# Attention weights transposed by one DMA inside SBUF instead of by two through DRAM, and the last merge's weights loaded once for both token tiles

## The chip, the cores and the metric

One Trainium2 chip; the same program runs on 8 of its cores, each core on one batch entry (2048 tokens of 1024 channels). The metric is device time in microseconds of the slowest core. Names of engines: PE is TensorE (matmuls), ACT is ScalarE, DVE is VectorE, POOL is GpSimd, SP is SyncE. DMAs that SP issues go to one queue, those that POOL issues to another; both are served by the core's 16 DMA engines.

## The reference, cut to what matters

Two layers; each has a mixer of three gated branches and then a feed-forward block. Here is what the change touches: the attention branch, whose weights w are the difference of two softmaxes, and the gated sum of the branches.

```python
for l in range(DEPTH):
    h = rmsnorm(x, norm_mix_pre[l])
    z = h @ w_in[l]                                  # za | zq | zk | zv | zc | zg
    ya = gmlp_branch(...)
    # branch B, 4 heads, causal: two score maps for each head
    p = jax.nn.softmax(sc, axis=-1)                  # (B,H,2,Q,S)
    w = p[:, :, 0] - lam * p[:, :, 1]                # (B,H,Q,S)
    yb = rmsnorm(einsum('bhqk,bkhe->bqhe', w, v), subln_g) * (1 - lambda_init)
    yc = pool_branch(...)
    up = einsum('bsnw,nwd->bsnd', stack([ya, yb, yc], 2), w_branch[l])
    gates = sigmoid(zg)
    merged = sum(gates * up, axis=2)
    x = x + rmsnorm(merged @ w_out[l], norm_mix_post[l])
    x = x + rmsnorm((silu(g) * u) @ w_ffn_out[l], norm_ffn_post[l])   # g, u from rmsnorm(x) @ w_ffn_in[l]
```

## The kernel before

**Order of work.** The program is written by a planner in Python (class `Sched`, function `emit`): every piece of work is a generator that yields what it needs, and the planner appends the piece that it reckons ready first, by its own durations, to the engine's list. Each engine then runs its list in order and waits on semaphores. So what stands in front of a matmul on PE is fixed beforehand, and a DMA that is later than the planner reckoned stops PE. Streams have priorities: the products with V (`pv_stream`), the scores (`qk_stream`), the output projection (`w_out`), and then the main stream, which fills the rest.

**Attention.** A step is one block of 128 queries (`qb`) of one head; a layer has 64 steps, in the order `ORDER` of blocks, 4 heads each. A step's width is w = (qb+1)*128 keys, from 128 to 2048. PE makes the scores, ACT their exponentials into the rings P (6144 columns, `ring1`) and P2 (3840 columns), DVE scales P2 and adds it to P. The result has queries on partitions, and the product with V needs keys there. `softmax` therefore writes it to DRAM (`wd`, 12 slots) with a DMA of SP, waits, and reads it back with a DMA that transposes blocks of 128 by 128 into the ring WT (8192 columns, `wring`). `pv_stream` gives the product with V a place on PE at the earliest 5 us (`LAG["pv"]`) after the planner's landing time. `finish` normalises a query block, transposes it on PE and sets the flag `("B", l, qb)`.

**Merging.** A slab holds the weights of a gate and a branch for 128 output channels (`dc`, 0 to 7). `gated` makes 8 matmuls for the gate and 4 for the branch, for one tile of 512 tokens. Slabs go through a ring of three slots WS, filled by DMAs of POOL that convert f32 to bf16; `acquire` and `release` count them, and a load is issued when its slot is released. Tokens are in two halves of 1024 and a half has two tiles. While attention runs, the main stream merges; its last part is the attention branch of the second half: tile 1 for `dc` 0 to 7, then, once all query blocks are done (flags B), tile 0 in two pieces (`merge_b` three times). Each of these calls loads its slabs `wb` anew. `load_wo` loads the output projection's weights wo by 8 DMAs on the same POOL list, when the last transposing DMA (flag `("W", l, 63)`) has been planned. SP loads the gains and the rows xr of the residual at that point as well. Then come `w_out` for the first half, tile 0 of the merge as filler, `w_out` for the second half and the feed-forward block (weights wfi through WS, wfo in one piece).

Of the kernel before, what the change touches and what calls it, by code (L numbers as in the profile page):

```python
# [18 lines left out]
L = 2  # L19
# [9 lines left out]
NWD = 12  # L29
# [197 lines left out]
def emit(nc, loads, T):  # L227
# [527 lines left out]
    def branch_b(sl):  # L755
        return v3(sl[:, 0:1024], 8), v3(sl[:, 1024:1536], 4)

    def merge_all(l, half, tag, dcs):
        for dc in dcs:
            ga, ba, gc, bc = branches(acquire(dr["wac"][l, dc], 3072))  # L760
            gb, bb = branch_b(acquire(dr["wb"][l, dc], 1536))
# [22 lines left out]
    def merge_b(l, half, tag, dcs, tiles=(0, 1)):  # L784
        for dc in dcs:
            sl = acquire(dr["wb"][l, dc], 1536)
            gb, bb = branch_b(sl)
            for tile in tiles:
                s = yield from gated(l, half, tile, gb, bb, YQ[half], bflags(l, half, tile), tag)
                dve("tensor_tensor", out=m_view(half, dc, tile * 512, (tile + 1) * 512), in0=mp_view(dc, tile * 512, (tile + 1) * 512),  # L790
                    in1=tt[:, s, :], op=ALU.add)
                ttfree.append(s)
            release()


    P, WT, wd = X["P"], X["WT"], dr["wd"]
# [62 lines left out]
    def softmax(l, i, t, off, n, s, wide, pos, ls):  # L859
# [10 lines left out]
        for c in range(2):  # L870
            src = ps[:, c:c + 3:2, 0:n // 2] if wide else bank(2 * s + c)[:, 0:n]
            yield "act", Need(reads=[src])
            dst = (P, P2)[c][:, pos[c] + off:pos[c] + off + n]
            act(dst.rearrange("p (b n) -> p b n", b=2) if wide else dst, src, AF.Exp, accum=l12[:, h, c:c + 1] if last and t == 0 else lq[:, c, t:t + 1])
# [14 lines left out]
        yield "sp", Need(reads=[p1])  # L889
        k = i % NWD  # L890
        S.dma("sp", f"WO{i % 4}", wd[k, :, 0:w], p1, [p1], [100 + k], w * 256)
        ring1.free(pos[0], w)
        yield "sp", Need(reads=[100 + k], cond=lambda: 0.0 if wring.place(w) is not None else INF)
        wp = wring.take(w)
        seg = WT[:, wp:wp + w]
        S.dma("sp", f"WI{i % 4}", seg.rearrange("p (k q) -> p k q", q=128), wd[k, :, 0:w], [100 + k], [seg], w * 256, transpose=True)
# [3 lines left out]
    def pv_stream(l):  # L900
        for i, (qb, h) in enumerate(steps()):
# [3 lines left out]
            def cond(i=i, w=w):  # L905
                wp = att[("w", i)]
                return S.ready([WT[:, wp:wp + w]]) + LAG["pv"]
# [7 lines left out]
            wring.free(wp, w)  # L915
            if h == 3:
                spawn(finish(l, qb))

# [3 lines left out]
    def finish(l, qb):  # L922
# [19 lines left out]
        rel(b)  # L942
        yield "pe", Need(nb=1, reads=[yt])
# [56 lines left out]
    def load_wo(l):  # L1000
        yield "pool", Need(flags=[("W", l, 63)])
# [16 lines left out]
    def ffn_in(l, half, tag):  # L1018
        for jp in range(11):
            sv = acquire(dr["wfi"][l, jp], 4096).rearrange("p (k a c) -> p k a c", k=8, a=2)  # L1020
            if half == 0:
                d = wfo[:, 2 * jp:2 * jp + 2, :].rearrange("p a c -> p (a c)")
                S.dma("pool", f"WF{jp}", d, dr["wfo"][l, jp], [], [d], 1048576)
# [33 lines left out]
    def main():  # L1057
        for l in range(L):
# [32 lines left out]
            flags.add(("hfree", ft))  # L1091
            yield from merge_b(l, 1, tag, range(4), (0,))
# [43 lines left out]
def build_program():  # L1136
# [6 lines left out]
        "wb": din("wb", [L, 8, 128, 1536]),  # L1143
# [16 lines left out]
        "wd": nc.dram_tensor("wd", [NWD, 128, S_LEN], BF16, kind="Internal").ap(),  # L1160
# [54 lines left out]
    assert place("wo", [2, 8, 512], BF16, a + 3 * 8192) <= e1  # L1215
# [94 lines left out]
```

How the kernel before makes its waits and increments, by code:

```python
            def body(e, en=en):  # L1249
                for waits, fn, key, inc in S.q[en]:
                    for k, v in waits:
                        e.wait_ge(sems[k], v)
                    if fn is not None:
                        fn(e).then_inc(sems[key], inc)
```

## Time and profile before

| | us |
|---|---|
| median of 3 runs (2303.27 to 2309.12) | 2305.35 |
| the profiled execution | 2321.07 |
| its span on the slowest core (core 3) | 2319.5 |
| spans of the 8 cores | 2285.3 to 2319.5 |
| PE busy | 2144.7 |
| DVE busy | 1093.1 |
| ACT busy | 936.3 |
| mean granted clock of TensorE on that core | 0.975 |

The span goes from the first to the last instruction of a core; the time of the profiled execution is 1.6 us longer. Busy time of PE counts overlapping matmuls once, so span less busy time is the time in which PE had nothing to run. A granted clock of 1 is 2.4 GHz, of 0.5 it is 1.2 GHz.

### The profile page before, as it was taken

The page shows a single profiled execution, that of the slowest core. Times are in us where ns is not written, and L with a number is a line of the kernel's source. Part 1 is how long each engine was busy: PE and PEld are TensorE (multiplying, and loading weights), DVE is VectorE, ACT ScalarE, POOL GpSimd, SP SyncE. Part 2 cuts the span into 40 slices and gives each one's busy share as a digit, 9 for nine tenths or more (in the row PEclk, how much of TensorE's full clock was granted, in tenths as well). Part 3 has the DMA queues.
Part 4 walks back from the last instruction along what each step waited for, and adds up shares of the span by engine and source line. Part 5 has one row for each costly group of instructions (what it writes and reads, how often), then busy time and mean ns, then how long its engine had stood idle before and what let it go on. Part 6 is the DMA issues. An engine that isn't in the chain of part 4 may idle for free.

```text
span 2319.5 us, 37223 instructions; the slowest of 8 cores (2285.3 to 2319.5 us)
## 1 busy us (share of the span) xinstructions
PE 2144.7 (92%) x11360; PEld 981.6 (42%) x11360; DVE 1093.1 (47%) x2129; ACT 936.3 (40%) x2322; POOL 435.3 (19%) x740
## 2 busy tenths in 40 slices
PE   5997899899589999999999989898978999999998
PEld 2443344334244444444444434344433444444443
DVE  4557667556267223322334676476654742232223
ACT  4456667564145113211333566575633531111111
POOL 3431111112132111111113311111122321101100
PEclk9999999999799999999999999999998999999999
DMA  9755777887888983455335458688876997516401
GB/s 217 100 77 105 129 140 153 134 135 131 167 183 201 166 118 85 108 84 73 84 67 77 85 112 137 109 153 149 152 161 151 214 205 118 106 64 137 73 28 64
DMA packets 258753, 287.10 MB, mean 124 GB/s; under 512 B 157824, under 2 KB 171136, under 8 KB 258560
## 3 DMA queue, kind: packets, MB, share of 16 engines
q0 software_dynamic: 73728, 132.38, 39.4%
q1 hardware_dynamic: 184832, 152.35, 25.3%
q8 instruction: 97, 1.59, 0.3%
q14 instruction: 96, 0.79, 0.1%
HBM read 312.15 MB, written 69.21 MB: 164 GB/s over the span
## 4 chain that ended last, share of the span: by engine, by line
PE 73%; DMA 17%; DVE 4%; issue 3%; SPq 2%; ACT 1%; POOL 1%; DVEq 0%; POOLq 0%; ACTq 0%
PE ps L289 72%; DMA wd<-P 6%; DMA WT<-wd 5%; DMA WS<-wb 3%; SPq L187 2%; PE ps L286 1%; DMA WS<-wfi 1%; DMA xr<-x 1%; DVE st L274 1%; DMA WS<-wmix 1%; DVE y L274 0%; DMA wsT<-wsT 0%; DVE P_66 L274 0%; DVE vall L274 0%; DVE P L274 0%
## 5 line engine op out<-in xcount | busy, mean ns | idle before, releaser
L289 PE MATMUL ps<-hT,WS 128*128 128x512 bf16 x5120 | 1165.6, 381 | 57.9 <-DMA WS<-wb 48.8
L289 PEld LDWEIGHTS ps<-hT,WS 128*128 128x128 bf16 x5120 | 488.4, 98 | 649.9 <-issue 100.2
L252 ACT ACTIVATE tt<-ps 128x512 f32<-128x512 f32 x368 | 219.9, 598 | 723.1 <-PE ps L289 718.8
L274 DVE TENSOR_TENSOR aT<-ps,tt 128x512 bf16<-128x512 f32 x176 | 121.7, 692 | 443.5 <-PE ps L289 438.9
L289 PE MATMUL ps<-wfo,aT 128*128 128x512 bf16 x1408 | 306.5, 379 | 0.0
L274 POOL TENSOR_TENSOR st<-st,nh 128x1 f32<-128x1 f32 (+1 forms) x192 | 120.8, 633 | 909.9 <-DVE st L274 888.2
L274 DVE SCALAR_TENSOR_TENSOR tt<-tt,ps 128x512 f32<-128x512 f32 x192 | 131.7, 686 | 237.0 <-PE ps L289 212.7
L289 PE MATMUL ps<-WS,hT 128*128 128x512 bf16 x768 | 186.5, 388 | 22.9 <-DMA WS<-wmix 10.6
L289 PEld LDWEIGHTS ps<-wfo,aT 128*128 128x128 bf16 x1408 | 137.3, 98 | 163.3
L289 PE MATMUL ps<-y,WS 128*128 128x512 bf16 x768 | 202.7, 387 | 0.2 <-DVE tt L274 0.2
L252 ACT ACTIVATE P<-ps 128x512 bf16<-128x512 f32 (+3 forms) x320 | 169.6, 531 | 50.5 <-PE ps L289 37.4
L252 ACT ACTIVATE P_66<-ps 128x512 bf16<-128x512 f32 (+3 forms) x320 | 170.6, 535 | 36.1 <-DVE P L274 10.9
L189 POOL DMA_DIRECT2D WS<-wfi x176 | 93.4, 538 | 401.2 <-PE ps L289 378.3
L252 ACT ACTIVATE junk<-ps 128x512 bf16<-128x512 f32 x128 | 76.4, 597 | 189.6 <-PE ps L289 184.8
L289 PE MATMUL ps<-V,WT 128*128 128x128 bf16 x1088 | 85.8, 226 | 49.9 <-DMA WT<-wd 44.7
L289 PE MATMUL ps<-KT,y 64*128 64x512 bf16 (+3 forms) x640 | 112.4, 359 | 5.0 <-ACT P_66 L252 4.5
L289 PEld LDWEIGHTS ps<-WS,hT 128*128 128x128 bf16 x768 | 71.2, 99 | 107.4 <-issue 38.1
L274 DVE TENSOR_SCALAR st<-st 128x1 f32<-128x1 f32 x160 | 26.6, 174 | 181.3 <-ACT junk L252 177.3
L274 DVE SCALAR_TENSOR_TENSOR t<-ps,st,gpost 128x512 f32<-128x512 f32 x128 | 95.6, 747 | 32.3 <-POOL st L274 31.4
L289 PEld LDWEIGHTS ps<-y,WS 128*128 128x128 bf16 x768 | 69.1, 99 | 89.8 <-issue 21.7
L289 PEld LDWEIGHTS ps<-V,WT 128*128 128x128 bf16 x1088 | 71.0, 101 | 81.0 <-issue 65.6
L274 DVE TENSOR_TENSOR P<-P,P_66 128x128 bf16<-128x128 bf16 (+15 forms) x128 | 92.8, 725 | 13.4
(90 smaller groups left out, 1696.0 us busy)
## 6 DMA issues: line engine op xcount, KB each, us to landing
WS<-wfi POOLq DMA_DIRECT2D x176, 256.0 KB, 7.5
WS<-wmix POOLq DMA_DIRECT2D x96, 256.0 KB, 8.1
WS<-wac POOLq DMA_DIRECT2D x96, 256.0 KB, 6.7
xs<-xr SPq DMA_DIRECT2D x48, 512.0 KB, 3.1
xr<-xs SPq DMA_DIRECT2D x48, 512.0 KB, 9.9
xr<-x SPq DMA_DIRECT2D x32, 512.0 KB, 12.7
WS<-wb POOLq DMA_DIRECT2D x48, 256.0 KB, 5.4
wfo<-wfo POOLq DMA_DIRECT2D x22, 512.0 KB, 11.9
```

Source lines behind the costliest of these rows:

```text
L187: fn = lambda e: e.dma_start_transpose(out, in_)
L189: fn = lambda e: e.dma_start(out=out, in_=in_)
L252: S.op("act", lambda e: e.activation(**kw), aps(in_, scale, bias), w, dur)
L274: S.op(eng, lambda e: getattr(e, method)(**kw), ins, w, dur)
L286: ins = e.transpose(it[1], it[2], it[3])
L289: ins = e.matmul(o, lh, rh, start=s, stop=p, skip_group_check=True)
```

## The change

1. `softmax` no longer writes to `wd`: one DMA of SP transposes from the ring P straight into WT. It waits for the step before it to have been planned (flag `("W", l, i - 1)`), and takes 128 columns more of the ring than it fills (`WPAD`). The exponentials' planning now also asks for their place in P to be free (`writes=[dst]`).
2. `pv_stream` starts a new query block only while at most one other is unfinished (`obank`), and sets a flag `("pv", l)` at its end.
3. The slabs `wb` are stored in pairs of 3072 columns. `merge_b_last` loads the four pairs of the last merge once: three into WS, where they stay for both tiles, and one into a buffer of its own, `wbx`. Tile 1 of all pairs comes first, then tile 0.
4. `load_wo` waits for `("pv", l)`, since wo now lies where V was. The order in which the pieces of `wfo` are loaded changes, since that region overlaps too.

```diff
-NWD = 12
+WPAD = 128
...
+    def merge_b_last(l, tag, ft):
+
+        pairs = [(2, acquire(dr["wb"][l, 2], 3072)), (3, acquire(dr["wb"][l, 3], 3072)), (0, acquire(dr["wb"][l, 0], 3072)), (1, X["wbx"][:])]
+        for i in range(0, 3072, PIECE):
+            d = X["wbx"][:, i:i + PIECE]
+            S.dma("pool", f"WX{i}", d, dr["wb"][l, 1, :, i:i + PIECE], [], [d], PIECE * 512)
+        for tile in (1, 0):
+            for n, (p, sl) in enumerate(pairs):
+                for i in range(2):
+                    yield from merge_b(l, 1, tag, 2 * p + i, (tile,), sl[:, i * 1536:(i + 1) * 1536])
+                if tile == 0:
+                    if n < 3:
+                        release()
+                    if n == 1:
+                        flags.add(("hfree", ft))
+            if tile == 1:
+                yield Need(flags=[("B", l, qb) for qb in range(16)])
+                gains("gpost", l, 1)
+                gains("gpre", l, 2)
+                open_banks()
+                stream(w_out(l, 0, ft), 4)
...
+            yield "act", Need(reads=[src], writes=[dst])
...
-        yield "sp", Need(reads=[p1])
-        k = i % NWD
-        S.dma("sp", f"WO{i % 4}", wd[k, :, 0:w], p1, [p1], [100 + k], w * 256)
+        yield "sp", Need(reads=[p1], flags=[("W", l, i - 1)] if i else [], cond=lambda: 0.0 if wring.place(w + WPAD) is not None else INF)
+        wp = wring.take(w + WPAD)
+        seg = WT[:, wp:wp + w]
+        S.dma("sp", f"WI{i % 4}", seg.rearrange("p (k q) -> p k q", q=128), p1, [p1], [WT[:, wp:wp + w + WPAD]], w * 256, transpose=True)
         ring1.free(pos[0], w)
-        yield "sp", Need(reads=[100 + k], cond=lambda: 0.0 if wring.place(w) is not None else INF)
-        wp = wring.take(w)
-        seg = WT[:, wp:wp + w]
-        S.dma("sp", f"WI{i % 4}", seg.rearrange("p (k q) -> p k q", q=128), wd[k, :, 0:w], [100 + k], [seg], w * 256, transpose=True)
         att[("w", i)] = wp
         flags.add(("W", l, i))
...
-            def cond(i=i, w=w):
+            def cond(i=i, w=w, h=h):
+                if h == 0 and len(obank) > 1:
+                    return INF
...
-            wring.free(wp, w)
+            wring.free(wp, w + WPAD)
             if h == 3:
                 spawn(finish(l, qb))
+        flags.add(("pv", l))
...
-        yield "pool", Need(flags=[("W", l, 63)])
+        yield "pool", Need(flags=[("pv", l)])
...
-            yield from merge_b(l, 0, tag, range(4))
+            yield from merge_b_first(l, tag)
             yield from pool_branch(l, 1, tag)
             yield from merge_ac(l, 1, tag, range(8))
+            ft = f"f{l}"
             spawn(load_wo(l))
-            yield from merge_b(l, 1, tag, range(8), (1,))
-            yield Need(flags=[("B", l, qb) for qb in range(16)])
-            gains("gpost", l, 1)
-            gains("gpre", l, 2)
-            open_banks()
-            ft = f"f{l}"
-            stream(w_out(l, 0, ft), 4)
-            yield from merge_b(l, 1, tag, range(4, 8), (0,))
-            flags.add(("hfree", ft))
-            yield from merge_b(l, 1, tag, range(4), (0,))
+            yield from merge_b_last(l, tag, ft)
...
-    assert place("wo", [2, 8, 512], BF16, a + 3 * 8192) <= e1
+    assert place("wo", [2, 8, 512], BF16, r) <= a
+    assert place("wbx", [3072], BF16, a + 3 * 8192) <= e1
```

SP during attention of the first layer, where the steps of 2048 keys follow those of 1024, in the kernel before:

```order
L189 DMA wd<-P 128x1024
L187 DMA_TRANSPOSE WT<-wd 128x8x128
L189 DMA wd<-P 128x2048
L187 DMA_TRANSPOSE WT<-wd 128x16x128
L189 DMA wd<-P 128x2048
L187 DMA_TRANSPOSE WT<-wd 128x16x128
```

The same place on SP with the change, from the steps of 640 keys to those of 2048 (x4 is one row for the four heads):

```order
L187 DMA_TRANSPOSE WT<-P 128x5x128 x4
L187 DMA_TRANSPOSE WT<-P 128x6x128 x4
L187 DMA_TRANSPOSE WT<-P 128x7x128 x4
L187 DMA_TRANSPOSE WT<-P 128x8x128 x4
L187 DMA_TRANSPOSE WT<-P 128x16x128 x4
```

Of two DMAs for each step one is left, and no row stands between two transposing DMAs.

POOL at the end of the first layer's attention, in the kernel before: the last slab of the other branches (wac), then slabs of the attention branch (wb) in two pieces each, and wo:

```order
L189 DMA WS<-wac 128x1024 x3
L189 DMA WS<-wb 128x1024
L189 DMA WS<-wb 128x512
L274 TENSOR_TENSOR st<-st,nh 128x4
L189 DMA WS<-wb 128x1024
L189 DMA WS<-wb 128x512
L189 DMA WS<-wb 128x1024
L189 DMA WS<-wb 128x512
L189 DMA wo<-wo 128x1024 x8
L189 DMA WS<-wb 128x1024
L189 DMA WS<-wb 128x512
```

The same place on POOL with the change, where a slab of wb is three pieces:

```order
L189 DMA WS<-wac 128x1024 x6
L274 TENSOR_TENSOR st<-st,nh 128x4
L189 DMA WS<-wb 128x1024 x6
L274 TENSOR_TENSOR st<-st,nh 128x4
L189 DMA WS<-wb 128x1024 x3
L189 DMA wbx<-wb 128x1024 x3
L189 DMA wo<-wo 128x1024 x8
```

The 8 DMAs of wo have moved from between the slabs to behind all of them, and the slabs that tile 0 used to load again are gone.

PE from the first layer's last product with V (the row with V,WT) to the first matmul with wo, in the kernel before; hT,WS x8 with y,WS x4 is one gated piece of 12 matmuls, and ident,yt is the transpose in `finish`:

```order
L289 MATMUL ps<-V,WT 128x128 x9
L289 MATMUL ps<-hT,WS 128x512 x8
L289 MATMUL ps<-y,WS 128x512 x4
L286 MATMUL ps<-ident,yt 128x128 x4
L289 MATMUL ps<-hT,WS 128x512 x8
L289 MATMUL ps<-y,WS 128x512 x4
...
L289 MATMUL ps<-hT,WS 128x512 x8
L289 MATMUL ps<-y,WS 128x512 x4
L289 MATMUL ps<-wo,ma 128x512 x128
```

The same place on PE with the change, where two gated pieces read the buffer wbx:

```order
L289 MATMUL ps<-V,WT 128x128 x9
L289 MATMUL ps<-hT,WS 128x512 x8
L289 MATMUL ps<-y,WS 128x512 x4
L289 MATMUL ps<-hT,wbx 128x512 x8
L289 MATMUL ps<-y,wbx 128x512 x4
L289 MATMUL ps<-hT,wbx 128x512 x8
L289 MATMUL ps<-y,wbx 128x512 x4
L286 MATMUL ps<-ident,yt 128x128 x4
L289 MATMUL ps<-wo,ma 128x512 x8
L289 MATMUL ps<-hT,WS 128x512 x4
L289 MATMUL ps<-wo,ma 128x512 x4
```

Three gated pieces instead of six stand between the last product with V and the first matmul with wo; the other three now stand ahead of that product.

## Rows read from the trace of the kernel before

**Rows 1.** The page, busy us of each engine (share of the span) xinstructions.

```profile
PE 2144.7 (92%) x11360; PEld 981.6 (42%) x11360; DVE 1093.1 (47%) x2129; ACT 936.3 (40%) x2322; POOL 435.3 (19%) x740
```

**Rows 2.** Waits of PE, whole span: us in total, times, longest us.

```profile
PE ps L289 <- DMA WS<-wb: 48.8, 6, 24.4
PE ps L289 <- DMA WT<-wd: 44.7, 19, 8.3
```

**Rows 3.** Windows: attention of both layers, and the stall behind the first.

```profile
150.00:440.00 290.00, 264.51 (x1580) 118.69 (x1578) 191.68 (x439) 183.43 (x541) 47.91 (x72) 0.96 0.72 129
440.00:552.00 112.00, 99.31 (x597) 43.93 (x597) 68.63 (x146) 71.03 (x205) 13.89 (x23) 0.97 0.80 135
...
580.00:610.00 30.00, 3.29 (x18) 1.35 (x16) 3.47 (x7) 1.20 (x2) 2.13 (x3) 0.63 1.04 225
610.00:664.00 54.00, 54.00 (x250) 24.32 (x249) 33.48 (x57) 23.23 (x53) 15.50 (x29) 0.95 0.63 127
1300.00:1590.00 290.00, 257.54 (x1510) 114.45 (x1509) 184.97 (x422) 177.80 (x524) 46.80 (x71) 0.95 0.73 127
```

(Columns: length, then busy us and instructions of PE, PEld, DVE, ACT and POOL, granted clock, DMA share, GB/s.)

**Rows 4.** Waits of PE, 552 to 690 us, end of the first layer's attention.

```profile
PE ps L289 <- DMA WS<-wb: 27.2, 3, 24.4
PE ps L289 <- DMA WS<-wfi: 3.5, 1, 3.5
PE ps L286 <- DVE yt L274: 2.3, 1, 2.3
```

**Rows 5.** The same for the second layer, 1696 to 1890 us.

```profile
PE ps L289 <- DMA WS<-wb: 21.7, 3, 20.0
PE ps L286 <- DVE yt L274: 2.7, 1, 2.7
...
PE ps L289 <- DMA WS<-wfi: 1.4, 1, 1.4
```

**Rows 6.** Timeline of POOL: start us, us, instruction, idle before and releaser.

```profile
571.88 4.28 POOL L189 DMA_DIRECT2D wo<-wo  x8
```

**Rows 7.** The chain that ended last, in order of time: start us, us.

```profile
404.54 15.14 DMA WT<-wd
...
576.15 33.30 DMA WS<-wb
```

**Rows 8.** Timeline of PE from the first layer's last product with V.

```profile
579.34 0.66 PE L289 MATMUL ps<-V,WT 128*128 128x128 bf16 x9 [1.14 <-DMA WT<-wd]
...
609.69 3.57 PE L289 MATMUL ps<-hT,WS 128*128 128x512 bf16 x8 [24.38 <-DMA WS<-wb]
...
622.68 1.89 PE L289 MATMUL ps<-hT,WS 128*128 128x512 bf16 x8
```

**Rows 9.** Timeline of SP behind the first layer's last transposing DMA.

```profile
572.23 0.41 SPq L189 DMA_DIRECT2D gpost<-gains  x1
...
573.28 9.77 SPq L189 DMA_DIRECT2D xr<-x  x6
```

**Rows 10.** A window inside the stall; columns as in the windows above.

```profile
586.00:596.00 10.00, 0.00 (x0) 0.00 (x0) 0.00 (x0) 0.00 (x0) 0.00 (x0) 0.59 1.04 250
```

**Rows 11.** Waits of the SP queue: us in total, times, longest us.

```profile
SPq L1252 <- DMA wd<-P: 411.2, 107, 13.6
...
SPq L1252 <- PE ps L289: 3.2, 2, 2.4
```

**Rows 12.** Tile WT, 282 to 340 us (widest steps): issue ns, landing us.

```profile
L187 SPq DMA_TRANSPOSE WT<-wd x5: 1575/2165/3287, 285.4 to 333.8; - x5
...
DMA to landing us min/median/max: 4.6/4.9/9.3
```

**Rows 13.** DMA issues: KB each, median us from issue to landing.

```profile
xr<-x SPq DMA_DIRECT2D x32, 512.0 KB, 12.7
...
wo<-wo POOLq DMA_DIRECT2D x16, 256.0 KB, 20.8
wd<-P SPq DMA_DIRECT2D x8, 480.0 KB, 4.1
```

More of the change, by code:

```diff
@@ L760, in merge_all @@
             ga, ba, gc, bc = branches(acquire(dr["wac"][l, dc], 3072))
-            gb, bb = branch_b(acquire(dr["wb"][l, dc], 1536))
+            gb, bb = branch_b(acquire(wb(l, dc), 1536))
             for tile in range(2):
@@ L782, in merge_ac, with merge_b, wb, merge_b_first @@
             release()
[L784 to L792, printed above, removed]
-            release()
-    P, WT, wd = X["P"], X["WT"], dr["wd"]
+    def merge_b(l, half, tag, dc, tiles, sl):
+        gb, bb = branch_b(sl)
+        for tile in tiles:
+            s = yield from gated(l, half, tile, gb, bb, YQ[half], bflags(l, half, tile), tag)
+            dve("tensor_tensor", out=m_view(half, dc, tile * 512, (tile + 1) * 512), in0=mp_view(dc, tile * 512, (tile + 1) * 512),
+                in1=tt[:, s, :], op=ALU.add)
+            ttfree.append(s)
+    def wb(l, dc):
+        return dr["wb"][l, dc // 2, :, dc % 2 * 1536:(dc % 2 + 1) * 1536]
+    def merge_b_first(l, tag):
+        for dc in range(4):
+            yield from merge_b(l, 0, tag, dc, (0, 1), acquire(wb(l, dc), 1536))
+            release()
+    def merge_b_last(l, tag, ft):
[18 more added lines that the diff above has]
+                stream(w_out(l, 0, ft), 4)
+    P, WT = X["P"], X["WT"]
     ring1, ring2, wring = Ring(P1RING), Ring(P2RING), Ring(WRING)
@@ L871, in softmax @@
             src = ps[:, c:c + 3:2, 0:n // 2] if wide else bank(2 * s + c)[:, 0:n]
-            yield "act", Need(reads=[src])
             dst = (P, P2)[c][:, pos[c] + off:pos[c] + off + n]
+            yield "act", Need(reads=[src], writes=[dst])
             act(dst.rearrange("p (b n) -> p b n", b=2) if wide else dst, src, AF.Exp, accum=l12[:, h, c:c + 1] if last and t == 0 else lq[:, c, t:t + 1])
@@ L942, in finish @@
         rel(b)
+        del obank[qb]
         yield "pe", Need(nb=1, reads=[yt])
@@ L1021, in ffn_in @@
             if half == 0:
-                d = wfo[:, 2 * jp:2 * jp + 2, :].rearrange("p a c -> p (a c)")
-                S.dma("pool", f"WF{jp}", d, dr["wfo"][l, jp], [], [d], 1048576)
+                z = (6, 7, 10, 0, 1, 2, 3, 4, 5, 8, 9)[jp]
+                d = wfo[:, 2 * z:2 * z + 2, :].rearrange("p a c -> p (a c)")
+                S.dma("pool", f"WF{z}", d, dr["wfo"][l, z], [], [d], 1048576)
             for jj in range(2):
@@ L1142, in build_program @@
         "wac": din("wac", [L, 8, 128, 3072]),
-        "wb": din("wb", [L, 8, 128, 1536]),
+        "wb": din("wb", [L, 4, 128, 3072]),
         "wo": din("wo", [L, 2, 128, 4096]),
@@ L1159, in build_program @@
         "xs": nc.dram_tensor("xs", [S_LEN, D], F32, kind="Internal").ap(),
-        "wd": nc.dram_tensor("wd", [NWD, 128, S_LEN], BF16, kind="Internal").ap(),
         "out": nc.dram_tensor("out", [S_LEN, D], F32, kind="ExternalOutput").ap(),
@@ L1276, in _pack @@
     wac = np.stack([np.stack([np.concatenate([gate(l, 0, d), gate(l, 2, d), br(l, 0, d), br(l, 2, d)], 1) for d in range(8)]) for l in range(L)])
-    wb = np.stack([np.stack([np.concatenate([gate(l, 1, d), br(l, 1, d)], 1) for d in range(8)]) for l in range(L)])
+    wb = np.stack([np.stack([np.concatenate([gate(l, 1, d), br(l, 1, d), gate(l, 1, d + 1), br(l, 1, d + 1)], 1) for d in range(0, 8, 2)]) for l in range(L)])
     wo = np.stack([np.stack([kslab(w_o[l][:, i * 512:(i + 1) * 512]).reshape(128, -1) for i in range(2)]) for l in range(L)])
```

## The prediction

> **What bounds the kernel now.** I read the page first. PE is busy 2144.7 us of the 2319.5 us span, and no other engine is busy for half of it [rows 1]. The change leaves the number of matmuls as it is, so it can only act on the 175 us in which PE stands still, and on the clock. The waits of PE show what they end with: slabs of the attention branch (WS<-wb) 48.8 us in six waits, transposed attention weights (WT<-wd) 44.7 us in nineteen [rows 2]. Half of PE's idle time ends with one of the two transfers that the change touches.
>
> The first is one long stall in each layer. PE waits 24.4 us for wb at the end of the first layer's attention [rows 4] and 20.0 us in the second layer [rows 5]. POOL's timeline shows why: the eight DMAs of wo are issued from 571.88 to 576.16 [rows 6], and the chain then runs for 33.30 us over a piece of wb issued right behind them [rows 7], which ends when PE starts again at 609.69 [rows 8]. Meanwhile SP has issued two gains and six rows of xr [rows 9], and the 16 DMA engines are full: share 1.04, 250 GB/s [rows 10]. So the stall is a queue: wb stands behind 6.3 MB of other loads.
>
> The second is spread over the attention. A step's weights are written to DRAM and read back, and SP waits 411.2 us in total for the writes, 107 times [rows 11], with the next step's DMA behind the waiting one. At the widest steps a transposing DMA lands 4.6 to 9.3 us after its issue, median 4.9 [rows 12], but the chain also holds one that took 15.14 us [rows 7].
>
> Both also cost clock. The granted clock is 0.95 to 0.97 in the attention windows and 0.63 where the long stall lies [rows 3]; the first 8 matmuls behind that stall take 3.57 us, where 1.89 us is usual [rows 8].
>
> **The change, part by part.** I sum against the profiled execution, 2321.1 us (1.6 us over its span). It lies 0.7% above the median of the runs, so the result is scaled by 2305.35/2321.07 = 0.9932.
>
> *The last merge.* All four pairs of wb are now issued ahead of wo, as slots of the branches before them come free, so 24.4 and 20.0 us of waiting go. The transpose in `finish` now has three gated pieces between the last product with V and itself, where there was one, so its waits of 2.3 and 2.7 us [rows 4, 5] go too: 49.4 us removed.
>
> A new wait takes part of that back. wo lies where V was, so its DMAs can start only behind the last product with V, and PE needs it soon: 3 gated pieces, 36 matmuls, later. At 54.00 us for 250 matmuls [rows 3] that is 7.8 us; 8 matmuls with wo and 4 of a gate later (2.6 us) it needs the second half of wo, at 10.4 us. PE's list is in order, so everything behind stands too: tile 0's merge, and the releases of slots that feed the first wfi loads. How late is wo? It is 8 x 256 KB, 2.1 MB landed [rows 13]; six rows of xr at 512 KB [rows 13] and two gains of the same size make 4.2 MB beside it. At 250 GB/s [rows 10] wo alone takes 8.4 us, all of it 25 us; I add 2 us for landing, an estimate. Lower bound: wo goes first and lands after 10.6 us, no wait. Upper bound: everything goes first, 27 us, a wait of 17. Before, SP issued the gains 7.1 us ahead of the last product with V (572.23 against 579.34) [rows 8, 9]; those 7.1 us move 1.8 MB, the other 4.5 MB take 18 us, and wo lands after about 20. I take a wait of 10 us for each layer, which also fits wo's median landing of 20.8 us [rows 13]. Sum of this part: -49.4 + 20 = **-29**, bounds -49 and -15. The slow matmuls behind a stall stay, since a wait of 10 us replaces it.
>
> *Slabs loaded once.* Behind the long stall PE waits again for wb and for the first wfi slab: 2.8 + 3.5 us in the first layer, 1.7 + 1.4 us in the second [rows 4, 5]. These wb loads no longer exist, and wfi can be issued when pair 2 is done, six gated pieces (15.6 us) before its use. I take **-8**; bounds 0 and -9.4.
>
> *One DMA instead of two.* For each of 128 steps a write of median 4.1 us at 480 KB [rows 13], and SP's wait for it, go. What a transpose from SBUF costs, no row shows. The nearest is the transpose from DRAM: issue 1.6 to 3.3 us, landing 4.9 us at the widest steps [rows 12]. It moves the same bytes and has no other reason in this trace to be slower or faster, so I take its durations. But this does not hand the whole write's time to PE. The planner reckons one DMA where it reckoned two and still adds 5 us, so it places the product with V earlier by about what is saved. What goes is the variance: of two transfers that weight loads can delay, and of SP's line, one is left. I therefore halve the 44.7 us [rows 2]: **-22**; bounds 0 (the delays are all of the transposing DMA) and -44.7. SP's new wait is for the sum in P; behind it stand the next transposes only, since rows of xr are loaded ahead of and behind attention.
>
> *The clock.* Shares lost in attention: 4% of 290 us, 3% of 112 us, 5% of 290 us [rows 3], 29.5 us in all, part of it in idle time. With half the stalls gone I take a third: **-10**; bounds 0 and -29.5.
>
> *At nothing:* the ring's 128 spare columns leave room for three steps of 2048 keys, where there were four; SP waited for PE 3.2 us in total before [rows 11], so the ring has not been short, and the cover is that a step's slot is needed for one landing and the planner's 5 us. P is held through a transpose of 4.9 us instead of a write of about 4; it has room for three of the widest steps. Holding back a new query block in `pv_stream` moves products with V later among the first, small blocks; other matmuls fill PE there, and without them the wait would be some us for each of three or four blocks.
>
> Sum: -29 - 8 - 22 - 10 = -69. 2321.1 - 69 = 2252, times 0.9932 gives **2236 us**. All lower bounds (-133) give 2173, all upper ones (-15) 2290.
>
> **The rivals.**
>
> *Only the tail gains.* The delays of WT come from weight loads that share the 16 engines (share 0.72 to 0.80 through the attention [rows 3]), not from the second DMA. Then the third and fourth terms are nothing: 2321.1 - 37 = 2284, scaled 2268. For it: the 15.14 us belonged to a transpose, not to a write. Against it: SP's 411.2 us.
>
> *wo eats the gain.* wo waits 17 us in each layer and attention stays, with another us or two of waiting for each held block at its start: 2306 + about 12 = 2318, scaled 2302, no measurable change. For it: DMA share 1.04 exactly there.
>
> *Slower: SP's queue becomes the pace.* A layer has 64 steps in about 429 us (150 to 579) [rows 3, 8], 6.7 us a step. If SP works off a transpose from SBUF piece by piece, its issue time grows with the width, and from a mean of 6.7 us a step SP sets the pace of attention: each us above it costs 128 us. The other 37 us are gone from 0.3 us above it. At a mean of 10 us: 2321 - 37 + 128 x 3.3 = 2706, scaled 2690. Against it: from DRAM even the widest steps are issued in 1.6 to 3.3 us [rows 12]; but that source is the one that goes.
> The Trainium skill (DMA: Bandwidth & Descriptors, section "Why a DMA increments its semaphore by 16 and not by 1", its table of sequencer times) speaks for this rival: in generations before the newest, a transpose from SBUF to SBUF pushes one command for each tile, 262,144 cycles for 8,192 tiles, 32 a tile. With the 256-byte tile of the same page's section "SDMA does more than copy", 128 steps have 139,264 tiles; at the SyncEngine's 1.2 GHz (Trainium Kernel Development and Optimization, section "NeuronCore Architecture") that is an estimate of 3,714 us of SP for the kernel, 29 us a step, and a time over 5,000 us. The table does not say how large its tile is, and with tiles of 4 KB it would be 1.8 us a step and no bound. No run here shows it yet.
>
> **How the numbers follow.** Chances: forecast 0.63 (its own range 2205 to 2265), only the tail 0.17, no change 0.06, slower 0.14. The last has little evidence in the trace, but no row excludes it. A difference of 0.3% (7 us) is about what a measurement of this kernel can tell from none: faster 0.80, same 0.06, slower 0.14. The range reaches from the forecast's lower bounds taken in part, 2203, to the no-change case, 2302; it leaves out the slower case and a few in a hundred below.
>
> **What would show it.** Right: no wait of PE for wb over 3 us; a new one for wo near 10 us in each layer; waits for WT (now <-P) near 22 us in all; SP's transposes issued in 1 to 3.5 us; clock 0.97 or more in attention. Wrong: issue times of SP that grow with the width to 7 us and more; waits for WT at every wide step; a wait for wo under 3 or over 17 us.

## The result, and the profile after

| | before | after |
|---|---|---|
| runs, us | 2303.27 to 2312.3 | 2230.49 to 2232.82 |
| the profiled execution | 2321.07 | 2232.82 |
| its span (core) | 2319.5 (3) | 2231.1 (4) |
| mean granted clock on that core | 0.975 | 0.990 |

The ratio is 0.9672, 95% interval 0.9646 to 0.9698: some 76 us faster. In two of the five runs of the change (2267.81 and 2514.93 us) the clock of a whole die was lower, which happens with either kernel; such runs are left out, here and below.

The waits of PE over the whole span, which answer to [rows 2] (us in total, times, longest us):

```profile
PE ps L289 <- DMA wo<-wo: 19.1, 6, 5.2
PE ps L289 <- DVE y L274: 12.8, 21, 1.7
PE ps L289 <- DMA WT<-P: 12.1, 3, 6.2
```

The 48.8 us for wb are gone. Of the 44.7 us for WT 12.1 are left, nearly all in two waits. The wait for wo is new. These are the end of attention in each layer, 552 to 690 us and 1630 to 1800 us, which answer to [rows 4, 5]:

```profile
PE ps L289 <- DMA wo<-wo: 7.1, 3, 5.0
...
PE ps L289 <- DMA wo<-wo: 12.0, 3, 5.2
PE ps L289 <- DMA WT<-P: 5.3, 1, 5.3
```

The timeline of PE from the first layer's last product with V, as in [rows 8] (start us, us, instruction, idle before and releaser):

```profile
562.57 0.67 PE L289 MATMUL ps<-V,WT 128*128 128x128 bf16 x9
...
570.84 0.39 PE L286 MATMUL ps<-ident,yt 128*128 128x128 bf16 x4
576.24 1.86 PE L289 MATMUL ps<-wo,ma 128*128 128x512 bf16 x4 [5.01 <-DMA wo<-wo]
579.00 1.86 PE L289 MATMUL ps<-wo,ma 128*128 128x512 bf16 x4 [0.90 <-DMA wo<-wo]
...
583.77 1.02 PE L289 MATMUL ps<-wo,ma 128*128 128x512 bf16 x4 [1.20 <-DMA wo<-wo]
```

The last product with V ends at 563.24 us; before it was at 580.00 [rows 8]. Behind it three gated pieces run without a stop; the first wait for wo ends 13 us after that product, where the wait for wb ended 30 us after it (609.69), and the last one after 20.5 us. On POOL the loads of wo are issued half a microsecond behind that product, with nothing of wb behind them (as [rows 6]):

```profile
549.34 1.60 POOL L189 DMA_DIRECT2D wbx<-wb  x3
563.78 4.24 POOL L189 DMA_DIRECT2D wo<-wo  x8 [12.83 <-PE ps L289]
```

Three of the windows of [rows 3] again (length, busy us of PE, PEld, DVE, ACT, POOL, granted clock, DMA share, GB/s):

```profile
150.00:440.00 290.00, 263.22 (x1598) 120.74 (x1627) 194.89 (x442) 186.32 (x544) 49.27 (x75) 0.98 0.61 90
440.00:552.00 112.00, 110.58 (x647) 49.89 (x659) 74.44 (x161) 74.77 (x221) 19.09 (x31) 1.00 0.70 106
...
1300.00:1590.00 290.00, 276.30 (x1702) 127.65 (x1735) 198.47 (x416) 195.12 (x561) 45.64 (x72) 0.99 0.64 98
```

The clock is up from 0.96, 0.97 and 0.95, and the bytes moved in the first from 129 to 90 GB/s. (219 matmul records of the span are missing from this trace, so busy times of PE are a little low.) SP's waits and its queue, as in [rows 11]:

```profile
SPq L1274 <- DVE P L274: 763.4, 124, 103.8
...
SPq L1274 <- PE ps L289: 4.7, 3, 2.4
...
q1 hardware_dynamic: 166400, 116.69, 20.8%
```

SP now waits for the sum in P, which is just its work running out; the 411.2 us for the write are gone. Its queue moves 116.69 MB where it moved 152.35. What a transpose from SBUF costs is in tile WT. First the six narrowest steps (147 to 163 us; four of 128 keys, two of 256), then mostly the widest (263 to 340 us), as [rows 12]: issue ns min/median/max, landing us.

```profile
L187 SPq DMA_TRANSPOSE WT<-P x6: 1100/1183/1419, 147.5 to 160.0; - x6
...
DMA to landing us min/median/max: 2.3/2.6/6.8
```

```profile
L187 SPq DMA_TRANSPOSE WT<-P x8: 1232/1890/4761, 266.4 to 335.8; - x8
...
DMA to landing us min/median/max: 3.0/4.9/11.9
```

At the median that is what the transposes from DRAM took (issue 1.6 to 3.3 us, landing 4.9 [rows 12]). The longest issue of the whole trace is 4.95 us; the prediction's sign had 1 to 3.5. Last, from the chain that ended last, its four longest transfers of WT and wo (start us, us):

```profile
394.94 17.64 DMA WT<-P
566.38 17.25 DMA wo<-wo
...
1635.61 15.81 DMA WT<-P
1655.83 23.31 DMA wo<-wo
```

Two single transposes that took four times the median of 4.0 us, and wo in each layer: this is most of what is left of the 93.5 us (48.8 and 44.7) for wb and WT.

### The profile page after: what moved, and what is told of

It reads as the page before. It is cut to its first block, busy times and chain, and to the rows that moved or that the text cites. A ratio compares the mean times of both kernels' runs of the same rounds, so it can differ in the third digit from the quotient of the medians.

```text
span 2231.1 us, 36572 instructions; the slowest of 8 cores (2215.9 to 2231.1 us)
## 1 busy us (share of the span) xinstructions
PE 2109.4 (95%) x11141; PEld 977.6 (44%) x11360; DVE 1089.8 (49%) x2128; ACT 935.3 (42%) x2323; POOL 415.8 (19%) x700
## 3 DMA queue, kind: packets, MB, share of 16 engines
q1 hardware_dynamic: 166400, 116.69, 20.8%
## 4 chain that ended last, share of the span: by engine, by line
PE 86%; DMA 5%; DVE 4%; issue 3%; ACT 1%; POOL 0%; DVEq 0%; POOLq 0%; ACTq 0%; SPq 0%
PE ps L289 84%; DMA WT<-P 2%; DMA wo<-wo 2%; PE ps L286 1%; DMA WS<-wmix 1%; DVE st L274 1%; DVE y L274 1%; DVE P_66 L274 0%; DVE vall L274 0%; DVE tt L274 0%; DVE ps L274 0%; ACT P L252 0%; ACT P_66 L252 0%; DVE P L274 0%; DVE h L274 0%
## 5 line engine op out<-in xcount | busy, mean ns | idle before, releaser
L289 PE MATMUL ps<-hT,WS 128*128 128x512 bf16 x4932 | 1135.4, 380 | 21.5 <-DVE y L274 4.9
L289 PEld LDWEIGHTS ps<-hT,WS 128*128 128x128 bf16 x5056 | 478.3, 98 | 597.7 <-issue 60.7
L289 PE MATMUL ps<-WS,hT 128*128 128x512 bf16 x740 | 179.3, 384 | 20.7 <-DMA WS<-wmix 10.6
L289 PE MATMUL ps<-y,WS 128*128 128x512 bf16 x718 | 186.1, 380 | 5.3 <-DVE y L274 3.0
L252 ACT ACTIVATE junk<-xr 128x1024 bf16<-128x1024 f32 x64 | 67.5, 1055 | 72.9 <-DVE xr L274 49.9
L274 DVE TENSOR_TENSOR xr<-xr,t 128x512 f32<-128x512 f32 x128 | 88.7, 693 | 13.7 <-DVE t L274 0.5
```

What stands on the lines that cost most here:

```text
L252: S.op("act", lambda e: e.activation(**kw), aps(in_, scale, bias), w, dur)
L274: S.op(eng, lambda e: getattr(e, method)(**kw), ins, w, dur)
L289: ins = e.matmul(o, lh, rh, start=s, stop=p, skip_group_check=True)
```

## The experiments

The theory behind the prediction has two parts: the last merge stops waiting because wb no longer stands behind wo, and attention stops waiting because, of two transfers that can be late, the write goes and only the transpose is left. The main rivals: only the first part gains, since the delays of WT come from weight loads; and SP's queue becomes the pace. Times are medians, ratios are to the kernel before in the same set.

| run | us | ratio [95%] | wait for WT | for wo |
|---|---|---|---|---|
| the change | 2232.2 | 0.9672 [0.9646, 0.9698] | 12.1 | 19.1 |
| t_only | 2264.1 | 0.981 [0.9757, 0.9863] | 22.0 | – (wb 21.0) |
| m_only | 2281.4 | 0.988 [0.9791, 0.9969] | 42.5 | 11.2 |
| dram_lag5 | 2291.9 | 0.9956 [0.9914, 0.9999] | 40.0 | 18.6 |
| write_kept | 2252.0 | 0.9754 [0.9698, 0.981] | 26.2 | 19.4 |
| thin_loads | 2219.8 | 0.9617 [0.9566, 0.9668] | 1.6 | 15.7 |
| wo_early | 2227.5 | 0.9652 [0.9587, 0.9716] | 22.2 | none (wbx 4.9) |
| wbx_early | 2224.8 | 0.9642 [0.9597, 0.9687] | 7.6 | 9.0 |
| wo_half | 2218.6 | 0.9616 [0.9545, 0.9687] | 11.4 | 12.1 |
| lag8 | 2219.3 | 0.9616 [0.9569, 0.9663] | none | 14.9 |
| lag11 | 2232.4 | 0.9699 [0.9676, 0.9722] | none | 14.9 |
| dram_lag8 | 2271.7 | 0.9879 [0.9843, 0.9916] | 29.3 | 14.5 |
| wo_half_lag8 | 2211.7 | 0.9613 [0.9597, 0.963] | 4.4 | 4.9 |

### Each part alone

**t_only** is the kernel before with the direct transpose (with its order of steps, hold and spare columns) and the old merge and wo:

```diff
-        S.dma("sp", f"WO{i % 4}", wd[k, :, 0:w], p1, [p1], [100 + k], w * 256)
...
+        S.dma("sp", f"WI{i % 4}", seg.rearrange("p (k q) -> p k q", q=128), p1, [p1], [WT[:, wp:wp + w + WPAD]], w * 256, transpose=True)
...
-        S.dma("sp", f"WI{i % 4}", seg.rearrange("p (k q) -> p k q", q=128), wd[k, :, 0:w], [100 + k], [seg], w * 256, transpose=True)
```

> The kernel before with the transposes from SBUF alone (with the spare columns and the hold on new query blocks that the planner needs for it); the last merge, its slab loads and wo are those of before. Theory (two separate gains, the attention's from fewer and earlier transfers): the attention loses the 33 us between its first scores and last product with V that the profiles differ by, plus the 16 us of merge work that the change moved ahead of that product, so 40 to 48 us faster than before, ratio 0.979 to 0.983; PE's waits for WT 10 to 20 us, its long wait for wb still 20 to 24 us in each layer. Rival (only the tail gains, the delays of WT come from weight loads): within 10 us of before, waits for WT 35 us or more. Rival (the parts need each other, because earlier attention only runs into the same queue of loads): 10 to 25 us faster, with the wait for wb grown to 30 us or more.

**m_only** is the changed kernel with those lines the other way round (the way through DRAM as it was before, without the new order and hold).

> The changed kernel with the weights again written to DRAM and read back transposed; the last merge is the changed one (slabs loaded once, wo behind the last product with V). Theory: 36 to 44 us faster than before, ratio 0.981 to 0.985; no wait for wb over 3 us, waits for wo 15 to 25 us in all, waits for WT 35 to 50 us as before. Rival (only the tail gains): 65 us faster or more, ratio 0.972 or less. Rival (the parts need each other): under 25 us faster, since wo's wait grows to 15 us a layer or more.

t_only took some 40 us off, as the theory expected; that alone refutes the rival by which the second DMA is hidden. But its waits missed: 20 to 24 us for wb were expected in each layer, and 10 to 20 for WT. Its waits over the span, then those around the end of the second attention (1640 to 1890 us):

```profile
PE ps L289 <- DMA WT<-P: 22.0, 4, 11.7
PE ps L289 <- DMA WS<-wb: 21.0, 5, 17.8
```

```profile
PE ps L289 <- DMA WT<-P: 11.7, 1, 11.7
...
PE ps L289 <- DMA WS<-wb: 2.3, 3, 0.9
```

The wait for wb stayed in the first layer only. In the second PE stood 11.7 us at the last product with V, and behind that hardly for wb. Of the 57.6 us between the two profiled spans (2319.5 and 2261.9) some 28 are therefore waiting for wb, which the theory had left in place; attention by itself, from the first score to the last product with V, became 26 us shorter in the two layers together, where the theory had 33. So t_only's time is not the price of the way through DRAM in attention alone. m_only took only 23 us off (28 by the ratio), where 36 to 44 were expected. Its waits show why:

```profile
PE ps L289 <- DMA WT<-wd: 42.5, 15, 11.4
PE ps L289 <- DMA wo<-wo: 11.2, 5, 4.4
```

No wait for wb is left, so the merge does what was forecast, and the wait for wo is 11.2 us where 15 to 25 were expected. But the waits for WT add up to what they were before, and the three longest have grown: 8.45 and 9.99 us at two products where PE waited 5.47 and 5.76 us before, and 11.39 us at the second layer's last product with V, where it was 0.57. PE at the longest, POOL and SP just ahead of it:

```profile
1680.47 1.12 PE L289 MATMUL ps<-V,WT 128*128 128x128 bf16 x9 [11.39 <-DMA WT<-wd]
```

```profile
1665.34 1.60 POOL L189 DMA_DIRECT2D wbx<-wb  x3
```

```profile
1659.76 0.51 SPq L189 DMA_DIRECT2D wd<-P  x1
1663.52 2.33 SPq L187 DMA_TRANSPOSE WT<-wd  x1
```

The loads of the last merge now fall on the last steps of attention. What was late is the transpose: in all three cases the write had landed 3.6 to 5.6 us after its issue, and the transposing DMA took 16.8 to 20.6 us. So each part takes something from the other's place; the rival that the parts need each other had the time right (under 25 us off), though not its reason (15 us for wo in each layer). By the medians the two alone add up to 63 us of 72 (by the ratios to 71 of 76, and their intervals do not exclude that nothing is missing).

### What the way through DRAM costs

**dram_lag5** puts back nothing but that way; order, hold and spare columns stay.

```diff
...
-        yield "sp", Need(reads=[p1], flags=[("W", l, i - 1)] if i else [], cond=lambda: 0.0 if wring.place(w + WPAD) is not None else INF)
+        yield "sp", Need(reads=[p1], flags=[("O", l, i - 1)] if i else [])
+        k = i % NWD
+        S.dma("sp", f"WO{i % 4}", dr["wd"][k, :, 0:w], p1, [p1], [100 + k], w * 256)
+        ring1.free(pos[0], w)
+        flags.add(("O", l, i))
+        yield "sp", Need(reads=[100 + k], flags=[("W", l, i - 1)] if i else [], cond=lambda: 0.0 if wring.place(w + WPAD) is not None else INF)
...
```

> The changed kernel with the way through DRAM put back and nothing else: the order of the steps on SP, the hold on new query blocks and the spare columns of the changed kernel stay, which m_only had not. Theory (the second DMA with SP's wait for it is what m_only paid for): waits for WT of 30 to 45 us and 2267 to 2287 us, as m_only's 2282. Rival (a good part of m_only's loss came from steps that overtook each other without that order and hold): 2240 to 2260 us.

Measured 2279.9 to 2299.5 us, with 40.0 us of waits for WT (core 1). The waits are what the theory expected; the time is 5 us above its 2267 to 2287. The rival is out: order and hold gained nothing by themselves. On top of the new merge the direct transpose is worth 49 us (against m_only) to 59 (against this run by the medians, 65 by the ratios, whose intervals are wide); on top of the old one it was worth 40, about half of it at wb.

**write_kept** asks how much of that is traffic. It is the changed kernel with the old write issued behind each transpose, to a buffer that is never read; the order of work on the other engines is unchanged. The last line lets the planner reckon the write as done when the transpose is.

```diff
+        kd, T0, L0 = i % NWD, S.T["sp"], dict(S.link)
+        S.dma("sp", f"WO{i % 4}", dr["wd"][kd, :, 0:w], p1, [p1], [100 + kd], w * 256)
+        S.T["sp"] = T0
+        S.link.update(L0)
+        S.fin[f"WO{i % 4}"][-1] = S.fin[f"WI{i % 4}"][-1]
```

> The changed kernel, with one thing of the old way put back: behind each transposing DMA the DMA that writes P to DRAM is issued too, to a buffer that nothing reads, 35.7 MB in all. The order of the work on TensorE, VectorE, ScalarE and GpSimd is that of the changed kernel. The table m_only says that the old way costs; this asks whether by its traffic or by its second leg. Theory (the second leg, that is the wait of SP for the write and the later start of the transpose): the waits for WT stay under 20 us and the time within 8 us of the changed kernel's, 2232 to 2240 us. Rival (the traffic on the DMA engines): waits for WT of 25 to 40 us and 2247 to 2257 us.

The rival, traffic, had the numbers right: 2252 us, 20 us slower than the change. SP around the longest wait, then PE:

```profile
397.55 9.65 SPq L188 DMA_TRANSPOSE WT<-P  x1
407.30 0.81 SPq L190 DMA_DIRECT2D wd<-P  x1
408.31 12.65 SPq L188 DMA_TRANSPOSE WT<-P  x1
```

```profile
423.54 1.65 PE L290 MATMUL ps<-V,WT 128*128 128x128 bf16 x14 [14.36 <-DMA WT<-P]
```

Beside weight loads the transposes took 9.65 and 12.65 us just to be issued, and PE stood for 14.36 us. The first had no write in flight in front of it, the second had. So the write, without anyone reading what it wrote, costs some 20 us of the slowest core's time, of the 49 to 65. How much of this is traffic was not separated, because ACT does wait for it, before it fills P again:

```profile
ACT P L253 <- DMA wd<-P: 28.7, 5, 14.1
```

Its two longest such waits (14.1 and 11.6 us) lie beside PE's two longest for WT; with the change ACT waits 6.3 us in this way, for transposes. For traffic speaks that the chain at the longest wait goes through the transposing DMA issued at 397.55 us, which landed after 25.9 us, where it was 17.6 at the same place with the change. The rest is tied to the second leg and SP's wait for the write; it was not measured by itself.

### What is left of the waits for WT

**thin_loads** is the changed kernel in which the loads of wac and wb move an eighth of their columns, so that the merges of the three branches run with whatever weights the slots held.

```diff
...
+                y = z // 8 if src.tensor.name in ("wac", "wb") else z
+                dst = WS[:, m % NSLOT, a:a + y]
...
```

> The changed kernel, same instructions in the same order, but every DMA of a slab of the merges (wac, wb) moves only the first eighth of its columns, so the merges use stale weights for the rest: part of the computation is changed, for its time alone. Theory (what is left of the waits for WT, 12.1 us in three waits, is weight loads in the way of a transposing DMA): landings of WT stay under 9 us (17.6 us the longest now), waits for WT under 3 us, and the kernel is 10 to 20 us faster than the changed one. Rival (what is left comes from SP's queue or the ring of WT): landings and waits as now, within 5 us of the changed kernel.

The waits for WT fell from 12.1 to 1.6 us and the longest landing of a transpose from 17.6 to 9.4 us (under 9 was expected); 12 us came off the time. What still delays the transposes are weight loads on the other queue, as the rival about the tail had it. **wbx_early** moves three such loads only:

```diff
...
-            yield from merge_ac(l, 1, tag, range(8))
+            yield from merge_ac(l, 1, tag, range(2))
+            spawn(load_wbx(l))
+            yield from merge_ac(l, 1, tag, range(2, 8))
```

> The changed kernel with the three loads of wbx issued after the second of the eight weight columns of the merge that runs beside the last attention steps, instead of after all eight, so that they no longer stand among the loads in front of the last transposing DMAs. Theory (what is left of the waits for WT is weight loads that share the DMA engines with the transposes at the end of an attention): of the 5 to 6 us for which TensorE waits for WT at the end of the second attention most goes, and 5 to 8 us come off the time of the changed kernel, about 2224 to 2228 us. Rival (the loads of wb that stay are enough to hold the last transposes up): the wait for WT stays at 4 us or more and the time is within 3 us of the changed kernel's 2232.

The 5.28 us at the end of the second attention went, 6.03 us in the middle of the first attention, where no wbx is loaded, stayed (6.15 with the change), and 8 us came off, as the theory expected. The wait for wo fell to 9.0 us as well, which was not foreseen.

**lag8** leaves all loads and gives the late ones room:

```diff
-LAG = {"pv": 5.0, "pe": 0.7, "qk": 0.2}
+LAG = {"pv": 8.0, "pe": 0.7, "qk": 0.2}
```

> The changed kernel, planned with products with V 8 us later behind the planned landing of their transposed weights instead of 5. Theory (what is left of the waits for WT is single transposing DMAs that land up to 13 us late behind weight loads, which 3 us more of margin cover in part): waits for WT of 6 us or less instead of 12, and 0 to 8 us faster, 2224 to 2232 us. Rival (the margin fills the ring of WT, so that transposes are held back and the last products with V come later): waits for WT unchanged or the end of the attentions later, 2232 to 2245 us.

No wait for WT is left, and about 13 us came off, more than the theory's 8. **lag11** is the same with 11:

> As lag8, with 11 us. No wait for WT is left in lag8, so nothing is left for the margin to take. Theory (the margin only covers late landings, and the ring of WT has room): the same as lag8 within 5 us, 2214 to 2225 us. Rival (each us of margin pushes the end of attention back, and lag8 gained in spite of that): the last products with V come 3 us later in each layer than in lag8, 2223 to 2232 us.

2232.4 us, all of lag8's gain gone, as the rival had it, but not in even parts. From the first score to the last product with V the first layer takes 418.1 us (lag8 415.2), the second 424.3 (415.8); 3 and 9 us. Its waits of SP for PE, over the span:

```profile
SPq L1274 <- PE ps L289: 22.3, 3, 18.4
```

SP waited 18.4 us at once in the first attention for a place in the ring, 2.4 at most with the change. But SP waited in this way for 19.9 of the 22.3 us in the first attention, and not at all in the second, which lost more; there PE had 8 us more to do before its last product with V (410.6 us busy against 402.5), merge work that the plan had put ahead of it. Another 7 us went between the two attentions. So of the three margins tried 8 us is the best; why 11 loses is shown in part only, and that the length of the ring sets the optimum is not shown.

**dram_lag8** is dram_lag5 with the margin of 8. (For the kernel before with a margin of 8 the planner finds no complete order, so it has no time.)

> dram_lag5 with products with V 8 us behind the planned landing, as lag8 has it for the direct transpose (2219 us). Theory (the second DMA costs because transfers land late against the plan, which a margin covers, and write_kept puts some 20 us on its traffic): waits for WT of 5 to 20 us, and 2235 to 2258 us, so that the two ways differ by less than half as much more as the traffic explains. Rival (the way through DRAM also lacks slots and rings for a longer stay, so that the margin gives back nothing): within 8 us of dram_lag5 or slower.

Both missed. The margin took 20 us off here too (2271.7), so the way through DRAM does have room for it; but 52 us stay between the two ways at 8, against 59 at 5 (by the ratios 60 and 65), more than the 20 us of write_kept explain. Its waits of PE and SP:

```profile
PE ps L290 <- DMA WT<-wd: 29.3, 12, 8.0
...
SPq L1280 <- DMA wd<-P: 444.2, 102, 14.6
SPq L1280 <- DVE P L275: 297.0, 40, 103.9
```

SP still spends 444.2 us waiting for writes, single ones up to 14.6 us, and 3 us more of margin do not cover that. Its three longest waits (4.8 to 8.0 us) nonetheless end with transposes that landed 14.5 to 17.8 us after their issue. Of the 54.8 us between the two profiled spans (2270.9 and 2216.1) 29.3 are waits for WT, and the lower mean clock (0.981 against 0.988) is about 0.7% or 16 us.

### The wait for wo

**wo_early** puts wo back in its old place in y, loaded ahead of the end of attention, and wbx in K's place, loaded after the last scores.

```diff
-        yield "pool", Need(flags=[("pv", l)])
+        yield "pool", Need()
...
-    assert place("wo", [2, 8, 512], BF16, r) <= a
-    assert place("wbx", [3072], BF16, a + 3 * 8192) <= e1
+    assert place("wo", [2, 8, 512], BF16, a + 3 * 8192) <= e1
+    assert place("wbx", [3072], BF16, r) <= e1
```

> The changed kernel with wo in the place it had before (two of the y buffers that the merge of branch A has finished with), so that its loads don't wait for the last product with V; the fourth pair of slabs lies where K was and is loaded when the last scores are made. Theory (wo waits only because its place comes free late): the waits for wo, 19 us in the profile of the changed kernel, go to under 3 us, and with them some 5 us of half clock: 18 to 25 us faster than the changed kernel, ratio to before 0.956 to 0.960. Rival (the DMA engines are what is short there, not the place): wo moves into the end of the attention and delays the last transposes or the fourth pair by as much; waits for WT and wbx grow by 10 to 20 us, 0 to 8 us faster than the changed kernel.

The rival held. The waits of PE:

```profile
PE ps L289 <- DMA WT<-P: 22.2, 5, 9.1
...
PE ps L289 <- DMA wbx<-wb: 4.9, 3, 4.5
```

The 19.1 us for wo are gone; 10 more for WT and 4.9 for wbx came, and 5 us are left as gain. The eight loads only changed what they are in front of. **wo_half** loads the first half much earlier (behind the second of eight weight columns of the merge before) and the second half where the change has it:

```diff
+            spawn(load_wo(l, 0))
+            yield from merge_ac(l, 1, tag, range(2, 8))
...
+            spawn(load_wo(l, 1))
```

> The changed kernel with wo in two buffers: its first half takes a place of y that is free early and is loaded while attention still runs, its second half takes V's place after the last product with V, as before; wbx moves to another place of y. Theory (the new wait for wo is the time in which eight loads land, behind the last product with V; the first half is wanted first): the waits for wo fall from 19 us to 5 or less and 10 to 18 us come off, 2214 to 2222 us. Rival (the earlier load of half of wo holds up the last transposes, as in wo_early): the waits for wo fall, those for WT rise by as much as 8 us, and the time is within 6 us of the changed kernel's, 2226 to 2234 us.

The time is what the theory gave (2215.0 and 2222.2 us, two runs only), the waits only in part: 12.1 us for wo, not 5, because PE comes to the second half 8 matmuls (1.9 us) after the first, and its four loads, issued behind the last product with V, have not landed by then. **wo_half_lag8** joins it with the margin:

> wo_half and lag8 together. In wo_half the waits for wo were 12.1 us and one transpose of 10.5 us too late stopped TensorE; in lag8 no wait for WT was left, but 14.9 us for wo. Theory (two separate causes, so their gains add): waits for WT of 2 us or less, waits for wo of 8 to 12 us, and 5 to 12 us faster than lag8, 2207 to 2215 us. Rival (both take from the same slack of the DMA engines around the end of attention): the wait for wo is 13 us or more, or waits for WT come back with 4 us or more, and the time is lag8's, 2215 to 2225 us.

2210.5 to 2212.5 us, the fastest kernel here; its ratio, 0.9613 [0.9597, 0.963], lies clear of the change's interval, so it beats both kernels. Its waits:

```profile
PE ps L289 <- DMA wo<-wo: 4.9, 4, 2.2
...
PE ps L289 <- DMA WT<-P: 4.4, 3, 2.8
```

The wait for wo fell further than either expected, and a little for WT came back. By its time it is 8 us below lag8, by the ratio, whose reference differed by 5 us between the two sets, it is level; whether the gains add fully stays open.

## Why the prediction was right

The predicted 2236 us is 0.970 of the time before; measured was 0.967. By its steps:

- **The last merge, -29.** In the profile -30.3: the 49.4 us went and 19.1 for wo came, 7.1 and 12.0 where 10 was taken for each layer. The working (wo behind gains and rows of xr at 250 GB/s, 20 us to land) gives the right size for a layer's mean; the chain has 17.25 and 23.31 us for loads of wo.
- **Slabs loaded once, -8.** The four waits of [rows 4, 5] are gone, 9.4 us.
- **One DMA instead of two, -22, and the clock, -10: the terms that were too small.** The waits for WT fell by 32.6 us, to 12.1 and not 22; what the clock loses in the three attention windows fell from 29.5 us [rows 3] to 8.7 (2% of 290, 0% of 112, 1% of 290). Halving was the guess, and its reason does not fit the traces: it took write and transpose as two transfers that weight loads can delay alike, of which one is left. In the kernel before, the six longest waits for WT (3.6 to 8.3 us, 31.6 of the 44.7) all end with a transposing DMA that landed 10.0 to 15.8 us after its issue, while the step's write had landed in 2.7 to 6.6. Two of them in the chain (start us, us):

```profile
439.90 2.67 DMA wd<-P
442.74 13.58 DMA WT<-wd
...
1461.11 5.60 DMA wd<-P
1467.20 15.80 DMA WT<-wd
```

So the late leg was the transpose, and it stays; what went is the write in front of it. With that, the same lateness costs less: a landing of 11.90 us costs PE 0.64 us with the change, where one of 9.98, behind a write of 4.6 that SP had waited for, cost 3.75 before (issued at 265.08 us), and only two single transposes behind weight loads still cost more than 5. The experiments put this part at 49 us (m_only) to 59 (dram_lag5), or 40 (t_only, about half of it at wb), where both terms together were 32.
- **Why the sum still fits: in part luck.** The measured terms add up to 93 us and the two profiled executions differ by 88.3, against a sum of 69. The two small terms together are 21 us short. But the ratio makes only 76 us of it (0.0328 of 2321.1): 12 us are put down to that one execution of the kernel before, which lay 0.7% above the median. The prediction took its waits from that execution and scaled only the end time, so what the terms lacked came out as 7 us of the time, 0.3%, and not 24. (The sums of 2252 and 2706 us scale to 2237 and 2688, where 2236 and 2690 stand; that changes nothing.)
- **A transpose from SBUF costs what one from DRAM costs.** This was the step with no row under it, and it held: at the median 1.18 us to issue at 128 and 256 keys, 1.89 at mostly 2048, landing 2.6 and 4.9 us. The rival by which SP's queue becomes the pace needed 6.7 us a step and is disproved. So, for this chip, is the Trainium skill's figure as it was read there (DMA: Bandwidth & Descriptors, section "Why a DMA increments its semaphore by 16 and not by 1": 32 cycles for each tile from SBUF to SBUF), which with tiles of 256 bytes gave an estimate of 29 us a step; if its tile is 4 KB, the estimate of 1.8 us a step is near the mean issue here (1.69 us). A cost for each tile does not show either way: one block took 1.10 us at the least and sixteen 1.78.
- **Only the tail gains** is refuted by t_only in its time, and by dram_lag5 on top of the new merge. Its mechanism, weight loads on the same engines, is real and makes up what is left (thin_loads). **wo eats the gain** is refuted by size: 19.1 us, not 34.
- **At nothing.** The ring with its spare columns cost nothing: SP waited 4.7 us for PE, 3.2 before. Order and hold gained nothing alone (dram_lag5 against m_only). The hold could not be taken away by itself, since the planner then finds no complete order, so its price was not measured.

## What to carry to other kernels

When a hop through DRAM is removed, do not take the hop's DMA for free because nothing reads what it writes: such a write cost 20 us here, with transposes in its queue issued up to 13.34 us long. Size what remains by asking which leg was late and which landings exceed the plan's margin, not by halving. And a load that is moved away from one wait has to be checked for what it is now in front of: in t_only, m_only and wo_early the lateness in part only moved, from wb or wo to the transposes.

## What the runs showed of the hardware

A transposing DMA's issue time grows little with its width (at the least 1.10 us for one block of 128 keys, 1.23 for eight, 1.78 for sixteen), but stretches under load: up to 4.95 us with the change, 9.65, 12.65 and at most 13.34 us with the unread write. Landing goes with it, from a median of 4.0 to 17.6 us with the change and 25.9 us in write_kept. The Trainium skill (DMA: Bandwidth & Descriptors, section "Queues, rings and completion order") says that a DMA engine takes turns, packet by packet, between the queues that have work for it. The runs agree as far as they go: loads on POOL's queue lengthen a transpose on SP's (thin_loads). That a write on SP's own queue does so too rests on write_kept alone, where the 12.65 us stand behind such a write in flight and the 9.65 us beside weight loads only.

The granted clock follows a stall. In write_kept, around the wait of 14.36 us, in three windows (columns as above):

```profile
400.00:409.00 9.00, 9.00 (x51) 3.82 (x49) 5.97 (x11) 6.16 (x20) 1.60 (x3) 1.00 1.18 157
414.00:427.00 13.00, 3.46 (x20) 2.03 (x20) 0.00 (x0) 1.38 (x4) 0.00 (x0) 0.50 1.29 128
428.00:440.00 12.00, 11.93 (x91) 5.93 (x89) 8.44 (x18) 9.09 (x26) 1.42 (x1) 1.00 0.37 89
```

PE was busy up to the stall (it stands from 409.2 us) at 2.4 GHz; from 414 us it was granted 1.2 GHz, while it stood and for the first 3.46 us of its work behind it. So a wait costs more than its own length: between the spans of write_kept and the change lie 18.5 us; the waits for WT differ by 14.1, and the mean clock (0.987 against 0.990) makes about 7 (rough figures: together they are a little more).
